# A full-precision matmul of ones and 288 columns ahead of the first down tile of each later MLP group

## The reference

```python
x = x + mix @ w_out
u = rmsnorm(x, g2) @ w_up                        # 1024 -> 4096
x = x + jnp.square(jax.nn.relu(u)) @ w_down      # 4096 -> 1024
```

## Time and profile before

| | us |
|---|---|
| time before, median of 3 runs | 1327.87 |
| time of the profiled execution | 1326.88 |
| its span, first to last instruction | 1325.1 |
| TensorE busy in it | 1303.1 (98%) |
| VectorE, ScalarE, GpSimd busy | 898.9, 607.9, 60.9 |

### The profile page before, as it was taken

One profiled execution on the slowest core, in us unless ns is written; L12 is line 12 of the kernel. 1 busy time (PEld: TensorE's weight loads), 2 busy tenths in 40 slices (PEclk: granted clock), 3 DMA queues, 4 the chain that ended last, 5 costly groups with the idle time before them and its releaser, 6 DMA issues.

```text
span 1325.1 us, 24681 instructions
## 1 busy us (share of the span) xinstructions
PE 1303.1 (98%) x10011; PEld 1273.2 (96%) x10011; DVE 898.9 (68%) x1488; ACT 607.9 (46%) x1104; POOL 60.9 (5%) x43
## 2 busy tenths in 40 slices
PE   7999999999999999999999999999999999999998
PEld 7999899899999999999999998999999999999998
DVE  6766787788476475486666768867965845846734
ACT  6323334488256156165242333345852732732833
POOL 0000001000000000000610000000000000000032
PEclk9999999999999999999999999999999999999999
DMA  8322121223223232222252222212322322322322
GB/s 236 80 80 69 52 63 36 77 64 122 71 83 109 64 95 95 88 71 95 87 118 70 65 66 63 64 33 80 96 88 73 96 96 64 100 89 68 124 64 72
DMA packets 115630, 110.26 MB, mean 83 GB/s; under 512 B 18830, under 2 KB 109398, under 8 KB 115414
## 3 DMA queue, kind: packets, MB, share of 16 engines
q1 hardware_dynamic: 110256, 105.06, 26.2%
q10 hardware_dynamic: 5286, 3.97, 1.0%
HBM read 105.21 MB, written 3.81 MB: 82 GB/s over the span
## 4 chain that ended last, share of the span: by engine, by line
PE 88%; DVE 7%; ACT 3%; issue 1%; DMA 0%; SPq 0%; ACTq 0%; DVEq 0%
PE psum L1684 56%; PE psum L2002 8%; PE psum L2004 8%; PE psum L2003 8%; PE psum L1737 1%; PE psum L1826 1%; PE psum L1910 1%; PE psum L1919 1%; PE psum L1928 1%; DVE w_lo L1023 1%; PE psum L1881 1%; PE psum L1899 1%; ACT w_hi L540 1%; PE psum L1857 1%; PE psum L1853 1%
## 5 line engine op out<-in xcount | busy, mean ns | idle before, releaser
L1684 PE MATMUL psum<-hid_h,w_hi 128*128 128x288 f32 x1232 | 266.2, 297 | 0.0
L1684 PE MATMUL psum<-hid_l,w_hi 128*128 128x288 f32 x1232 | 263.7, 295 | 0.0
L1684 PE MATMUL psum<-hid_h,w_lo 128*128 128x288 f32 x1232 | 263.6, 295 | 0.0
L1684 PEld LDWEIGHTS psum<-hid_h,w_hi 128*128 128x128 f32 x1232 | 197.1, 188 | 0.6 <-issue 0.3
L1684 PEld LDWEIGHTS psum<-hid_l,w_hi 128*128 128x128 f32 x1232 | 197.4, 188 | 0.0
L1684 PEld LDWEIGHTS psum<-hid_h,w_lo 128*128 128x128 f32 x1232 | 197.2, 188 | 0.0
L1684 PE MATMUL psum<-xh,w_hi 128*128 128x288 f32 x800 | 178.4, 304 | 2.2 <-ACT x L585 1.9
L1569 DVE TENSOR_TENSOR tmp<-psum,rms 128x576 f32<-128x576 f32 x63 | 47.7, 758 | 185.9 <-PE psum L1684 185.8
L1684 PE MATMUL psum<-xh,w_lo 128*128 128x288 f32 x800 | 171.7, 295 | 0.0
L1684 PE MATMUL psum<-xl,w_hi 128*128 128x288 f32 x800 | 171.6, 295 | 0.0
L788 ACT ACTIVATE w_hi<-stage 128x1024 fp32r<-128x1024 f32 x64 | 67.8, 1059 | 219.0 <-PE psum L1684 218.2
(11 more groups left out here) (327 smaller groups left out, 2567.6 us busy)
## 6 DMA issues: line engine op xcount, KB each, us to landing
stage<-in_w_up SPq DMA_DIRECT2D x32, 1024.0 KB, 5.6
stage<-in_w_down SPq DMA_DIRECT2D x32, 1024.0 KB, 5.1
stage<-in_w_in SPq DMA_DIRECT2D x18, 1024.0 KB, 5.3
stage<-in_w_in SPq DMA_DIRECT2D x16, 256.0 KB, 4.5
stage<-in_w_out SPq DMA_DIRECT2D x8, 512.0 KB, 6.2
stage<-in_w_out SPq DMA_DIRECT2D x4, 1024.0 KB, 5.2
z<-in_x_prompt SPq DMA_DIRECT2D x4, 512.0 KB, 5.8
out<-z SPq DMA_DIRECT2D x3, 512.0 KB, 2.7
```

The costliest lines, as they stand in the source:

```text
L1684: ins = M(acc[t % 2][:, a, :], lhs(w), mov[:, k, a * HALF:(a + 1) * HALF], start=first and n == 0, stop=last and n == 2)
```

## The change

`down_tile` gets a third argument, `mark`. Where it is set, one matmul of plain float32 operands (the tile of ones by the second 288 columns of `ssum`) is issued behind the tile's waits for weights and banks, and ahead of its first block. It goes to the bank of the second half of the accumulator that the tile is about to fill. The tile's own first matmul into that bank starts a new sum there, so the result of the added matmul is overwritten. It is set for the first down tile of groups 1 to 3 in both layers, and not for group 0, which has `sum_squares` in that place. These are six added matmuls in all; nothing is removed, and no semaphore is waited for or raised by them.

```diff
-                def down_tile(g, i):
+                def down_tile(g, i, mark=False):
                     pe.wait_ge(s_lo, slot_m + 8 * g + i + 1)
                     if i >= 2:
                         pe.wait_ge(s_evac, tile_m + 8 * g + i - 1)
...
                     else:
                         pe.wait_ge(s_fd, UP * l + 4 * g + 6)
+                    if mark:
+                        M(acc[tile_m % 2][:, 1, :], ones, ssum[:, HALF:T], start=True, stop=True)
                     for k in range(KT):
                         if i == 0:
                             pe.wait_ge(s_hid, hid0 + 8 * g + k + 1)
...
                     for i in range(KT):
-                        down_tile(g, i)
+                        down_tile(g, i, i == 0)
                 if l == DEPTH - 1:
                     for pi in range(4):
                         up_pair(GROUPS - 1, pi)
                     for i in range(KT - 1):
-                        down_tile(GROUPS - 1, i)
+                        down_tile(GROUPS - 1, i, i == 0)
```

## The result

The changed kernel takes 1330.86 us (median of 13 runs, 1329.6 to 1331.67), the kernel before 1327.56 (13 runs beside them, 1327.09 to 1327.91). The ratio is 1.0024, its 95% interval 1.0016 to 1.0033: slower by 3.3 us, where 4.7 less were forecast. This is near the first rival's 1330.8. The profiled execution took 1329.60 us, in a span of 1327.8.

The account below looks back on a forecast made before the run. TensorE's matmul pace bounds the kernel, without waits in the down tiles. Gains of 3.1 + 0.94 + 0.61 = 4.7 us, added matmuls' cost included, taken from 1326.88 and 1327.87 gave 1322.2 and 1323.2; range 1322.2 to 1327.0.

Parts of the forecast that it names:

- first rival: Later groups' down tiles: pace does not change, the six matmuls only cost 2.9 us, giving 1330.8; chance 0.10.
- The cost of the added matmul: Ahead of later groups' first down tile: two passes, 0.485 us each time, all on the path; six are 2.9 us.
- the gain of a quick section: Later groups' 384 down matmuls: 50.41 us with the added matmul against 51.19, saving 0.78 us.
- its being carried into the gate tile: Layer 0 group 3 plus 48 gate-tile matmuls: 0.94 us less at the quicker pace, 0.78 if the gate tile stays slow.
- VectorE and GpSimd keeping up: Group 3: VectorE busy 28.2 and GpSimd 22.0 of 45 us, so 6.24 us for a tile is enough.
- The quicker pace runs down: Later groups: one matmul buys at least 192 quick ones, gaining 0.15 us a group, 1327.0 in all; chance 0.08.
- the quicker pace followed in every place where this operation is followed by L1684: Argument against the only-cost rival: full-precision 288-column matmuls ahead of L1684 always brought about 130 ns instead of 133.3.
- the last pass before the down tiles, the thing nearest to them, is the same: Ahead of the down tiles: argument that one added matmul serves like the two of `sum_squares`; no size given.
- a chance of 0.80: Chance given to the forecast that later groups take the quicker pace, and to the kernel being faster.
- one matmul is not two: Objection for the only-cost rival: the change adds one matmul where group 0 has two of `sum_squares`; no size given.
- the fillers that had stayed slow behind full-precision scores: Behind the attention scores, 36 fillers ran at 133.3 ns each, 130.0 behind four full transposes; evidence for the only-cost rival.
- 340 again: Sign of the only-cost rival: still 340 matmuls in 45 us of later groups' down tiles, not some 348.

Follow-up runs that it names:

- cycle_two: Kernel before, TensorE's groups written out, two full-precision 288-column matmuls behind 8 to 13 matmuls of each later group's second down tile; 1331.71 us (before 1327.01).
- narrow64: The changed kernel, loops kept, its added matmul 64 columns wide in place of 288; 1320.88 us, ratio 0.9952 to the kernel before.

## Why the prediction was wrong

**What was right.** The cost of the added matmul: forecast 0.485 us, measured 0.49, from two passes of 242 ns. All of it on the path; no new wait; up pairs unchanged; nothing else on any queue. And the gain of a quick section: 51.19 - 50.41 = 0.78 was forecast with one matmul of 0.485 inside. With the narrow one, which costs 0.22 us (50.14 less 384 x 0.130 = 49.92), the section came to 50.14. So the size of the quick pace, its lasting for 384 matmuls, its being carried into the gate tile, and VectorE and GpSimd keeping up all held. *The quicker pace runs down* fell with that.

**The step that failed** is the one that brought the quick pace to the later groups: "the quicker pace followed in every place where this operation is followed by L1684", and, of one against two, "the last pass before the down tiles, the thing nearest to them, is the same". Those rows came from very few places, all behind `sum_squares`, and all with two matmuls; they could not tell full precision from number, width or place. The runs show that the nearest pass doesn't decide: ahead of a down tile, behind the same last pass of 288 columns, two matmuls are quick, and one, three and four are slow. So in the later groups the six matmuls of the change left the pace at 133.3 ns, and only their 0.49 us each remained. The prediction named the objection, "one matmul is not two", and the fillers that had stayed slow behind full-precision scores. On these rows a chance of 0.80 was far too high for a gain that hangs on an unknown cause, where the cost was certain.

**That first premise was also not general.** In the changed kernel's own trace layer 1's first `sum_squares`, the two matmuls of the earlier trace rows, was followed by the slow pace from the start. The timeline there:

```profile
672.35 1.14 PE L1695 MATMUL psum<-ssum,io 128*128 128x288 f32 x4
...
673.59 0.43 PE L1684 MATMUL psum<-xl,w_hi 128*128 128x288 f32 x2
...
679.45 0.43 PE L1684 MATMUL psum<-xh,w_lo 128*128 128x288 f32 x2
```

From 673.59 to 679.45 lie 44 matmuls: 133.2 ns each, where the earlier trace rows had 130.2 for 44. The last three distances ahead of the four passes were 130, 131 and 133 ns here, and 132, 140 and 132 before: the four passes fell at another place of the cycle of four. `cycle_two` made such a difference by its edit, with the same effect, and the 38 cases of `sum_squares` above go by it without exception.

**The first rival** came true: the kernel was slower, "340 again" was there, the mark named ahead, and the sections of the trace show its price of 2.9 us. That its 1330.8 met the measured 1330.86 so closely is partly luck: the kernel before came out 0.3 us lower than the 1327.87 that it started from, and the difference of the medians 0.4 higher than 2.9. Its other half, that more matmuls only cost, is not general: `narrow64` adds six and is faster. The Trainium skill (TensorE: Matmul & The Clock Gate, section Back-to-back issue gap) gives the columns over 2.4 GHz plus 2.5 ns for a lone matmul at full clock, as an estimate 122.5 ns for 288 columns, and says that in a stream of weight loads and matmuls both set the distance. Here every matmul has a load of its own, and the trace agrees that the figure for a lone one is not the pace: it shows 130.0 or 133.3 ns.

**The range** of 1322.2 to 1327.0 left the first rival out at 0.10. The pace had two known values and an unknown switch; both sides of the switch belonged in it.

## What to carry to other kernels

Where one stream of equal matmuls runs at two paces in one trace, look at single distances, not at means: a repeating pattern (here 131, 131, 131, 140 against 128, 132) is a state that what comes ahead selects, and two matmuls that select one state at one place of the pattern select the other elsewhere. Such a state is to be tried with several fillers in one kernel, one for each repeat of the loop, before a rule is made of it; a cheap filler is worth the attempt, 64 columns in full precision for 0.22 us here. A gain that rests on a coincidence of two or three places in a trace, with no cause known, deserves no more than an even chance, and its range must hold the bare cost.

## What the runs showed of the hardware that was not expected

- TensorE has two lasting paces for the same stream of 288-column matmuls of the down tiles, at a granted clock of 1.00 with no wait: 130.0 and 133.3 ns. Both lasted for 336 to 432 matmuls without a switch in every section of down tiles that nothing was put into; another pace was seen only behind a pause or other work.
- Ahead of a later group, which one follows depends on what is added, in the same way wherever it was tried again. One full-precision matmul ahead of the tile was quick with 40, 56, 64, 72, 112, 120 and 128 columns, and slow with 32, 48, 80, 96, 136, 144, 160, 192, 256, 272, 280, 284, 288, 292, 296, 304 and 512. Two were quick with 256, 272, 284, 288, 296 and 320, and slow with 32, 64, 128 and 280. In the middle of a tile, the pair of 288 and the one of 64 also have to fall on one of four places.
- The same code can be followed by either pace: two matmuls of 288 at two places of the kernel were followed 15 times by the quick one and 23 times by the slow one, sorted by the place in the cycle of the stream ahead. Out of the quick pace they led to the slow one in 3 of 3.
- A full-precision matmul of up to 128 columns puts the stream back by 0.22 to 0.23 us whatever its width (in the quick cases 50.14 us for 40 as for 128 columns).
- Writing into another bank, even into one of the scores, changed nothing.

What in TensorE makes the two patterns, and why 80 columns or a pair of 280 fail between neighbours that work, stays open: no view shows the inside of its queue of loads and matmuls. The records of the weight loads show one difference. In the kernel before, in the slow pace (430 to 470 us), 75 of 300 loads took 192 ns, each at one of the long distances, and the others 187 or 188; in the quick pace (330 to 370 us) all took 187 or 188. In both, a load starts 2 to 4 ns behind the start of each matmul, so the records show no other order of loads and matmuls. Whether the longer load makes the long distance or follows from it is not shown.
